# Expert weights of a mixture-of-experts stage in four 4 MB slots instead of eight 2 MB slots

## What is computed

```python
def ec_moe(h, w_router, w_gate, w_up, w_down):
    B, T, D = h.shape
    cap = EC_CAPACITY_FACTOR * T // N_EXPERTS
    logits = jnp.einsum('btd,de->bte', h, w_router).astype(jnp.float32)
    aff = jax.nn.softmax(logits, axis=-1)
    gate, idx = lax.top_k(jnp.swapaxes(aff, 1, 2), cap)
    xs = jax.vmap(lambda hb, ib: hb[ib])(h, idx)
    a = jnp.einsum('becd,edf->becf', xs, w_gate)
    u = jnp.einsum('becd,edf->becf', xs, w_up)
    y = jnp.einsum('becf,efd->becd', jax.nn.silu(a) * u, w_down)
    y = y * gate[..., None].astype(y.dtype)
    return jax.vmap(lambda ib, yb: jnp.zeros((T, D), yb.dtype).at[ib.reshape(-1)].add(yb.reshape(-1, D)))(idx, y)
```

## Time and profile before

| | |
|---|---|
| median of three runs | 1639.85 us |
| the profiled execution, its own time | 1641.37 us |
| its span, from the first to the last instruction | 1639.7 us |
| TensorE busy | 1493.5 us, 91% of the span |
| VectorE, ScalarE, GpSimd busy | 454.4, 274.3, 54.0 us |
| moved by DMA | 566.07 MB, 345 GB/s over the span |
| DMA in 830 to 1420 us | 428 GB/s |
| loads of expert weights | 184 of 2 MB and 16 of 1 MB |

### The profile page before, as it was taken

One profiled execution on the slowest core, in us unless ns is written; L12 is line 12 of the kernel. 1 busy time (PEld: TensorE's weight loads), 2 busy tenths in 40 slices (PEclk: granted clock), 3 DMA queues, 4 the chain that ended last, 5 costly groups with the idle time before them and its releaser, 6 DMA issues.

```text
span 1639.7 us, 19983 instructions
## 1 busy us (share of the span) xinstructions
PE 1493.5 (91%) x8345; PEld 908.4 (55%) x8345; DVE 454.4 (28%) x876; ACT 274.3 (17%) x412; POOL 54.0 (3%) x90
## 2 busy tenths in 40 slices
PE   4559999999999999799999998998998999999888
PEld 2138888887788999643534334344344335335345
DVE  3244552435446744600030030030020110300202
ACT  3032222323233322400000000000000000000002
POOL 0001000000001000300000000000000000000000
PEclk8779999999999999899999999999999999999999
DMA  8978878786663435689999999999999999999996
GB/s 355 428 299 299 300 265 282 243 293 225 222 227 95 127 123 230 253 343 428 428 427 428 428 428 429 428 428 428 428 428 428 428 428 428 428 428 428 421 406 236
DMA packets 106363, 566.07 MB, mean 345 GB/s; under 512 B 7932, under 2 KB 62404, under 8 KB 72132
## 3 DMA queue, kind: packets, MB, share of 16 engines
q1 hardware_dynamic: 93424, 497.04, 74.3%
q0 software_dynamic: 9216, 67.11, 11.5%
q10 hardware_dynamic: 3668, 1.12, 0.3%
HBM read 561.84 MB, written 3.41 MB: 345 GB/s over the span
## 4 chain that ended last, share of the span: by engine, by line
PE 64%; DMA 30%; DVE 4%; issue 1%; ACT 1%; ACTq 0%; DVEq 0%; SPq 0%
PE psum L440 62%; DMA ring<-in_w_up 25%; DMA ring<-in_w_ada 3%; DMA ring<-in_w_in 1%; DVE w_parts L1164 1%; DVE hid L1415 1%; DVE mix L1342 0%; DMA hid<-in_b_ada 0%; DVE ring L1152 0%; PE psum L452 0%; PE psum L573 0%; ACT w_parts L877 0%; PE psum L838 0%; PE psum L860 0%; PE psum L777 0%
## 5 line engine op out<-in xcount | busy, mean ns | idle before, releaser
L440 PE MATMUL psum<-ring,hid 128*64 128x512 f32 (+1 forms) x3200 | 677.7, 578 | 68.5 <-DMA ring<-in_w_up 53.6
L440 PEld LDWEIGHTS psum<-ring,hid 128*64 128x64 f32 x3200 | 246.3, 137 | 482.4 <-issue 384.7
L440 PE MATMUL psum<-h_parts,w_parts 128*128 128x384 f32 x1152 | 212.5, 339 | 0.0
L440 PEld LDWEIGHTS psum<-h_parts,w_parts 128*128 128x128 f32 x1152 | 199.2, 188 | 16.6 <-issue 15.9
L877 ACT ACTIVATE hid<-psum 128x512 f32<-128x512 f32 (+5 forms) x104 | 62.9, 624 | 684.7 <-PE psum L440 471.7
L1491 DVE TENSOR_TENSOR hid<-psum,hid 128x512 f32<-128x512 f32 x16 | 11.1, 692 | 599.9 <-PE psum L440 599.9
L1164 DVE TENSOR_TENSOR w_parts<-ring,w_parts 128x2048 fp32r<-128x2048 f32 x52 | 119.2, 2291 | 120.6 <-ACT w_parts L877 120.0
L440 PE MATMUL psum<-ring,early 128*32 128x512 f32 (+1 forms) x780 | 116.7, 676 | 34.1 <-DMA ring<-in_w_ada 34.0
L877 ACT ACTIVATE w_parts<-ring 128x2048 fp32r<-128x2048 f32 x52 | 99.4, 1912 | 252.6 <-PE psum L440 194.6
L440 PEld LDWEIGHTS psum<-w_parts,h_parts 128*128 128x128 f32 x864 | 107.5, 195 | 28.1 <-issue 27.3
L440 PE MATMUL psum<-w_parts,h_parts 128*128 128x256 f32 x864 | 112.6, 290 | 8.7 <-DVE h_parts L1199 8.7
(11 more groups left out here) (165 smaller groups left out, 531.3 us busy)
## 6 DMA issues: line engine op xcount, KB each, us to landing
ring<-in_w_gate SPq DMA_DIRECT2D x64, 2048.0 KB, 32.9
ring<-in_w_up SPq DMA_DIRECT2D x64, 2048.0 KB, 25.8
ring<-in_w_down SPq DMA_DIRECT2D x56, 2048.0 KB, 34.0
ring<-in_w_ada POOLq DMA_DIRECT2D x64, 1024.0 KB, 5.2
ring<-in_w_in SPq DMA_DIRECT2D x36, 1024.0 KB, 5.2
ring<-in_w_ada SPq DMA_DIRECT2D x16, 2048.0 KB, 16.5
ring<-in_w_out SPq DMA_DIRECT2D x16, 1024.0 KB, 5.5
ring<-in_w_down SPq DMA_DIRECT2D x16, 1024.0 KB, 15.1
```

The source lines that it names most:

```text
L440: return nc.tensor.matmul(out, lhsT, rhs, start=start, stop=stop, skip_group_check=True)
```

## The change

The eight slots become four double slots (`WIDE`), which begin at the slots 4, 6, 2 and 0 (`WIDE_AT`). A matrix is now cut into halves of 4 MB, 12 to a pair, and a half is one transfer, in which partition p gets eight consecutive gate or up rows or four consecutive down rows, 32 KB contiguous in HBM and in SBUF. Three things keep the old size: the very first loads, which fill the four double slots in eight transfers of 2 MB, in the old order of slots and with the old waits (`FIRST_LOADS`); the products, which are the same in number and shape; and the down matrices of the last pair, which keep their 16 transfers of 1 MB and have semaphores of their own now (`last_landed`).

What changes with the halves is who waits for what. TensorE waits for a whole half before its first product, and `moe_used` rises when the whole half has been used, so that the next load into it is issued then. The counts that ScalarE and VectorE wait for are rewritten to mean the same points. In `rows_copy_out` the copies write runs of 64 columns instead of 128, and read with a step of 8 instead of 4, since the rows on a partition are eight now.

```diff
 MATS = [("g", 0), ("u", 0), ("g", 1), ("d", 0), ("u", 1), ("d", 1)]
-PER_PAIR = 4 * len(MATS)
+PER_PAIR = 2 * len(MATS)
 RING = 8
+WIDE = RING // 2
+LAST = PER_PAIR * (PAIRS - 1)
 FIRST_BANKS = [1, 2, 5, 6]
 LAST_BANKS = [2, 3, 0, 1]
-ORDER = [4, 5, 6, 0, 2, 3, 7, 1]
+WIDE_AT = [4, 6, 2, 0]
+FIRST_LOADS = [4, 5, 6, 0, 2, 3, 7, 1]
...
-        moe_landed = [sem(f"moe_landed{n}") for n in range(RING)]
+        moe_landed = [sem(f"moe_landed{n}") for n in range(WIDE)]
+        last_landed = [sem(f"last_landed{n}") for n in range(4)]
...
-            def expert_load(pair, q):
-                what, e = MATS[q // 4]
-                part, slot = q % 4, ORDER[q % RING]
+            def expert_load(pair, q, sub=None):
+                what, e = MATS[q // 2]
+                part, slot = q % 2, WIDE_AT[q % WIDE]
                 if what == "d":
-                    src = down_rows[bass.ds(pair * 2 * FF + e * FF + part // 2 * BLK, BLK), :]\
-                        .rearrange("(p j) n -> p j n", j=4)[:, part % 2 * 2:part % 2 * 2 + 2, :]
-                    dst = ring[:, slot, :].rearrange("p (k n) -> p k n", k=2)
+                    src = down_rows[bass.ds(pair * 2 * FF + e * FF + part * BLK, BLK), :].rearrange("(p j) n -> p j n", j=4)
                 else:
-                    src = (gate_rows if what == "g" else up_rows)[bass.ds(pair * 2 * D + e * D + part * 512, 512), :]\
-                        .rearrange("(p k) n -> p k n", k=4)
-                    dst = ring[:, slot, :].rearrange("p (k n) -> p k n", k=4)
-                sp.dma_start(dst, src).then_inc(moe_landed[slot], 16)
-            def last_down_load(q):
-                e, part, slot = MATS[q // 4][1], q % 4, ORDER[q % RING]
+                    src = (gate_rows if what == "g" else up_rows)[bass.ds(pair * 2 * D + e * D + part * 1024, 1024), :]\
+                        .rearrange("(p k) n -> p k n", k=8)
+                rows = src.shape[1]
+                dst = ring[:, slot:slot + 2, :].rearrange("p s n -> p (s n)").rearrange("p (k n) -> p k n", k=rows)
+                lo, hi = (0, rows) if sub is None else (sub * rows // 2, (sub + 1) * rows // 2)
+                sp.dma_start(dst[:, lo:hi, :], src[:, lo:hi, :]).then_inc(moe_landed[q % WIDE], 16)
+            def last_down_load(q, sub):
+                e, part, slot = MATS[q // 2][1], q % 2 * 2 + sub, WIDE_AT[q % WIDE] + sub
                 for half in range(2):
                     first = (PAIRS - 1) * 2 * FF + e * FF + half * BLK
                     src = down_rows[first:first + BLK, part * BLK:(part + 1) * BLK].rearrange("(p j) n -> p j n", j=4)
                     dst = ring[:, slot, half * 4 * BLK:(half + 1) * 4 * BLK].rearrange("p (j n) -> p j n", j=4)
-                    sp.dma_start(dst, src).then_inc(moe_landed[slot], 16)
+                    sp.dma_start(dst, src).then_inc(last_landed[part], 16)
...
-            for q in range(RING):
-                if ORDER[q] == 7:
+            for slot in FIRST_LOADS:
+                if slot == 7:
                     sp.wait_ge(ada_free, 2 + 64)
-                if ORDER[q] == 0:
+                if slot == 0:
                     sp.wait_ge(lo_ready, U_ALL)
-                if ORDER[q] == 2:
+                if slot == 2:
                     sp.wait_ge(unit_used, U_ALL)
-                if ORDER[q] == 3:
+                if slot == 3:
                     sp.wait_ge(logits_done, 1)
-                if ORDER[q] == 1:
+                if slot == 1:
                     sp.wait_ge(routed, 1)
                     sp.wait_ge(h2_pool, len(H2_POOL))
-                expert_load(0, q)
+                expert_load(0, WIDE_AT.index(slot // 2 * 2), slot % 2)
             with sp.Fori(0, PAIRS - 1) as i:
                 for j in range(PER_PAIR):
                     sp.wait_ge(moe_used, PER_PAIR * i + (j + 1))
-                    expert_load(i + (j + RING) // PER_PAIR, (j + RING) % PER_PAIR)
-            for j in range(PER_PAIR - RING):
-                sp.wait_ge(moe_used, PER_PAIR * (PAIRS - 1) + j + 1)
-                if MATS[(j + RING) // 4][0] == "d":
-                    last_down_load(j + RING)
-                else:
-                    expert_load(PAIRS - 1, j + RING)
+                    expert_load(i + (j + WIDE) // PER_PAIR, (j + WIDE) % PER_PAIR)
+            for j, used in ((0, 1), (1, 2)):
+                sp.wait_ge(moe_used, LAST + used)
+                expert_load(PAIRS - 1, j + WIDE)
+            for j, used in ((2, 3), (3, 4)):
+                sp.wait_ge(moe_used, LAST + used)
+                for sub in range(2):
+                    last_down_load(j + WIDE, sub)
+            for j, used in ((4, 5), (5, 6)):
+                sp.wait_ge(moe_used, LAST + used)
+                expert_load(PAIRS - 1, j + WIDE)
+            for j, used in ((6, 7), (7, 9)):
+                for sub in range(2):
+                    sp.wait_ge(moe_used, LAST + used + sub)
+                    last_down_load(j + WIDE, sub)
...
-            def up_or_gate(slot, what, e, part):
-                for kk in range(4):
-                    k = 4 * part + kk
+            def up_or_gate(slot, what, e, part, sub):
+                for kk in range(4 * sub, 4 * sub + 4):
+                    k = 8 * part + kk
                     for half in range(2):
-                        off = kk * FF + half * BLK
+                        off = kk % 4 * FF + half * BLK
                         last = mm(bank[0 if what == "g" else 1][ES * half:ES * half + ES, :],
-                                  xs[:, k, e * ES:(e + 1) * ES], ring[:, slot, off:off + BLK], k == 0, k == KC - 1)
+                                  xs[:, k, e * ES:(e + 1) * ES], ring[:, slot + sub, off:off + BLK], k == 0, k == KC - 1)
                 return last
             def down(slot, e, part):
-                for jl in range(2):
-                    half, j = part // 2, part % 2 * 2 + jl
-                    rows = actT[:, j * P + half * ES:j * P + (half + 1) * ES]
+                for j in range(4):
+                    rows = actT[:, j * P + part * ES:j * P + (part + 1) * ES]
                     for c in range(4):
                         row = ES * (c % 2 ^ e)
-                        off = jl * D + c * BLK
-                        last = mm(bank[2 + c // 2][row:row + ES, :], rows, ring[:, slot, off:off + BLK],
-                                  part == 0 and jl == 0, part == 3 and jl == 1)
+                        off = j % 2 * D + c * BLK
+                        last = mm(bank[2 + c // 2][row:row + ES, :], rows, ring[:, slot + j // 2, off:off + BLK],
+                                  part == 0 and j == 0, part == 1 and j == 3)
...
-            def landed(i, q, more=0):
-                pe.wait_ge(moe_landed[ORDER[q % RING]], 48 * i + 16 * (q // RING + 1 + more))
+            def landed(i, q):
+                pe.wait_ge(moe_landed[q % WIDE], 48 * i + 16 * (q // WIDE + 2))
             def round_of(i, first=False, last_pair=False):
                 for q in range(PER_PAIR):
-                    what, e = MATS[q // 4]
-                    part, slot = q % 4, ORDER[q % RING]
+                    what, e = MATS[q // 2]
+                    part, slot = q % 2, WIDE_AT[q % WIDE]
                     start = first and e == 0
                     if part == 0 and what == "g":
                         if e == 0 and not first:
@@ -793,14 +807,6 @@
                             pe.wait_ge(xs_act, 2 * i + 2)
                         if not start:
                             pe.wait_ge(sil_ready, 2 * i + e)
-                    if first and q < 4:
-                        for quarter in ([0, 1], [2], [3], [])[q]:
-                            gather_quarter(quarter)
-                        if q == 0:
-                            pe.wait_ge(mod_rows_out, N_MOD)
-                            turn_mod(bank[2], act)
-                        pe.wait_ge(xs_dve if q % 2 else xs_act, q // 2 + 1)
                     if part == 0 and what == "u" and not start:
                         pe.wait_ge(act_ready, 2 * i + e)
                     if part == 0 and what == "d":
@@ -812,17 +818,34 @@
                         if not start:
                             pe.wait_ge(y_out, 2 * i + e)
                         turn_act(i, e)
-                    landed(i, q, e + 1 if last_pair and what == "d" else 0)
-                    if what != "d":
-                        last = up_or_gate(slot, what, e, part)
-                    elif last_pair and e == 1:
-                        last = down_block(slot, e, part, bank[LAST_BANKS[part]][:, 0:UC])
-                    elif last_pair:
-                        last = down_block(slot, e, part, bank[2 + part // 2][:, part % 2 * UC:(part % 2 + 1) * UC])
+                    if last_pair and what == "d":
+                        for sub in range(2):
+                            block = 2 * part + sub
+                            pe.wait_ge(last_landed[block], 32 * (e + 1))
```

(38 more changed lines are left out.)

6 lines of the change are left out of this document (1 added, 5 removed).

## The result

The changed kernel takes 1643.10 us (median of 22 runs, 1640.98 to 1645.54), the kernel before 1640.23 in the same comparison (22 runs, 1638.99 to 1641.43). The ratio is 1.0017, with a 95% interval of 1.001 to 1.0023: 1.6 to 3.8 us slower. I had forecast 0.4 us less and no measurable change. The range held the time, the direction was wrong: a small loss that twenty runs can tell from nothing.

What follows compares the result with a forecast made beforehand. The prediction took the end to be set by the weight stream's start, its rate and TensorE's work after the last up landing. +2.7 + 3.4 - 6.5 = -0.4 us on 1639.85 gave 1639.4 us, range 1636.4 to 1646.1.

Steps and rivals of the forecast that it cites:

- the start: First loads that wait for TensorE: released later in halves, making the stream 2.7 us late; bounds 0 and 4.9.
- 2.9 us ahead of 724.1: Second half's issue at 721.24 against the first half's landing; claimed to leave no gap or 0.1 us.
- the latency of an idle queue: Start of the stream: 3.0 us, from 7.9 us to land a 2 MB load less 4.9 for its bytes.
- The packets: Weight stream up to the last up half: 32 KB packets replace 16 KB ones and gain 6.5 us.
- The rows' price for a packet: DMA queue: about 9.5 ns per packet beside its bytes, from rates with 2 KB and 16 KB packets.
- the 2.5 us estimated by that page: Stream gain from fewer packets by the skill's rule of some 3 cycles each; sum would be +3.6 us.
- The tail: Behind the last up landing TensorE has two quarters to do, so the end comes 3.4 us later.
- The remark that it has no cover: Tail: nothing hides the 3.4 us and no other wait is ahead of it.
- The middle: Mid-stream: coarser waits and releases cost nothing, with 12.7 us of cover where 3.0 are needed.
- The rival of a queue that runs dry between releases: Middle up loads: late TensorE releases empty the DMA queue; one us more gives +6.6, 1646.4 us, slower; chance 0.05.
- +2.7 + 3.4 - 6.5: Whole kernel: late start plus longer tail less the packets' gain, summing to -0.4 us.
- the chance of 0.57 for no change: Whole kernel: chance given to the forecast of -0.4 us, with its own range of 1636.6 to 1643.1.

Runs made afterwards that it cites:

- 10 to 12: Follow-ups second_quarters, pad60, pad35, second_pad60 and the control, on what makes the second half land late; 1642.88, 1641.81, 1643.14, 1640.42 and 1640.25 us.
- the control: Kernel before with 60 small transposes put at the start of TensorE's program; 1640.25 us, ratio 1.0000 to the kernel before.
- pad60: Changed kernel with 60 small transposes at the start of TensorE's program, shifting its later instruction fetches; 1641.81 us, ratio 1.0015 to the kernel before.
- second_quarters: Changed kernel with only the second half behind the initial loads released and loaded in quarters; 1642.88 us, ratio 1.0015 to the kernel before.
- before_start: Kernel before with the first four loads behind the initial ones issued in twos, after two quarters are used; 1644.04 us, ratio 1.0025.
- pad35: Changed kernel with 35 small transposes at the start of TensorE's program, shifting its later instruction fetches; 1643.14 us, ratio 1.0017 to the kernel before.
- second_pad60: Changed kernel with the second half behind the initial loads in quarters and 60 transposes at TensorE's start; 1640.42 us, ratio 1.0002 to the kernel before.
- both_quarters: Changed kernel with the first two halves behind the initial loads and the last expert's up matrix in quarters; 1634.56 us, ratio 0.9968 to the kernel before.
- Both mended kernels: both_quarters with 32 KB pieces, 1634.56 us, and both_pieces16 with 16 KB pieces, 1639.84 us.
- before_tail: Kernel before with TensorE waiting for two quarters at once only in the last expert's up matrix; 1643.73 us, ratio 1.0025.
- tail_quarters: Changed kernel with the last expert's up matrix loaded and waited for in quarters; 1639.24 us, ratio 0.9994 to the kernel before.
- eighths: both_quarters with the last up quarter in two 1 MB transfers, the second waited for separately; 1634.55 us, ratio 0.9963 to the kernel before.
- before_mid: Kernel before with TensorE waiting for two quarters at once in all pairs but the last, behind the first eight quarters; 1640.50 us, ratio 1.0002.
- both_pieces16: both_quarters with every 4 MB half in two 2 MB transfers, so pieces are 16 KB; 1639.84 us, ratio 1.0000 to the kernel before.

## Why the prediction was wrong

**The step that failed is the start.** It said that the second half is issued "2.9 us ahead of 724.1, just the latency, so it follows with no gap or one of 0.1", and that the stream is late by 2.7 us. The issue times were right, the gap was not. The stream is late by 3.3 to 4.3 us in the traces, and by 4.2 us (2.5 to 5.9) when the releases alone are made coarse.

What took the place of that step is shown by 10 to 12, each from one trace. The later release by itself costs about what was forecast: 2.5 us against the control with the same transposes (starts of 32.1 and 29.6), 2.0 against the 30.1 of before, which holds a fetch's delay of its own. On top comes a gap of 1.0 to 2.2 us. The first half lands 12.1 us behind its issue, not 12.7, so the lead was 2.3 us and not 2.9. The gap is there with that short lead and no fetch near (`pad60`, 1.9 us), and with a fetch at the seam and a longer lead (`second_quarters`, 1.4; `before_start`, lead of 3.0, 1.6); with a lead of 3.5 and a fetch inside the first half (`pad35`) it is 1.0. It is gone when both are away (`second_pad60`). So the forecast of this term had no place for the fetches, and where they fall was luck.

How much a short lead costs by itself is less sure. The prediction called its 3.0 us the latency of an idle queue, but the load of the earlier trace rows that it was read from was issued at 711.36, 1.6 us before the one ahead had landed (704.92 and 8.0). It needed 7.9 us; the load that did meet an idle queue, at 704.92, needed 8.0. With 2 MB in pieces of 16 KB a short lead cost nothing, then, in the kernel before or in the control. And in `both_quarters` a 4 MB load issued at 726.45, a lead of 3.0, landed 9.7 us behind the one ahead, with no gap (though one late engine had held up that landing, too). Only `pad60` speaks for a cost of the short lead, with 4 MB in pieces of 32 KB: 13.9 us from issue to landing, where 9.7 are its bytes and an idle queue needs 12.2. Why is open.

**The packets: right in kind, somewhat too high.** 6.5 us were forecast. Both mended kernels, with 32 and 16 KB pieces, are 5.3 us apart (some 2.5 either way, so 6.5 is not excluded), and the streams of the traces with large packets are shorter by 6.0 us, a mean of 859.7 in eleven against 865.7 in seven. The rate is the forecast's 431 to 432 GB/s and the step from half to half is 9.71 us. What is missing may go to landings that come late by themselves, such as one of 10.9 us behind the last in the changed kernel near 783, with a fetch in the same stretch. That the fetches cause them is argued from where they stand, and from `pad35`, whose first half was 1.2 us late with a fetch inside it.

The rows' price for a packet, 9.5 ns, was the better guide than the 3 cycles that the Trainium skill gives in "DMA: Bandwidth & Descriptors", section "Why small descriptors are slow (HBM only)": the 2.5 us estimated by that page are half of the 5.3 measured, and less than half of the 6.0 by which the streams differ.

**The tail: right.** 3.4 us forecast, 3.4 in the traces, 3.9 (2.5 to 5.6) by the time of `before_tail`, 3.5 to 3.9 back in `tail_quarters`. The remark that it has no cover is confirmed, and `eighths` shows how near the next wait was in the other direction.

**The clock: not foreseen.** In the profiled execution the first column block ran 1.7 us longer with part of it at the half clock. It is in two of the eight profiles with the coarse tail and 32 KB pieces (the changed kernel's and `pad35`'s, there in the last up half), and in `before_start`, whose tail is not coarse. So it belongs to that execution and not clearly to the change. In the middle the change does bring half-clock stretches, behind waits of about 2.5 us, and `before_mid` shows that they are free there.

**The middle: right.** Nothing that could be measured is lost to coarser waits and releases (`before_mid`, `both_pieces16`). The rival of a queue that runs dry between releases did not occur.

**The sum.** Measured one by one: 4.2 for the start, 3.9 for the tail, -5.3 for the packets, +2.8 together, where the changed kernel is 2.9 slower. Each of the three is known to some 1.5 to 2.5 us only, so that they meet the total this closely is partly luck; in the profiled executions the time from TensorE's first product on is 4.7 us longer in the first, with 1.7 of it the clock, and 1.0 in the second. The prediction had +2.7 + 3.4 - 6.5. Each term had the right sign, and all three errors go the same way: 1.5 us for the start, 1.2 for the packets, 0.5 for the tail. The start's is the largest, but had the start cost the 2.7 of the forecast, the measured terms would still add up to +1.3. With three terms that cancel to -0.4, errors of this size decide the sign; the chance of 0.57 for no change said little of that.

## What to carry to other kernels

Where a queue of transfers sets the end, look at its three parts by themselves: a larger transfer gains in the stream, but it is released later at the start and waited for whole at the end. Keep both ends in small pieces and take the large ones only in the middle; here that turned 2.9 us of loss into 5.3 of gain, with a version that beats both kernels. Where a load is to follow without a gap and its lead comes out within a microsecond of the latency, count a gap of 1 to 2 us as well: a fetch of instructions at the seam is enough for it. And before a latency is called that of an idle queue, look when the transfer ahead landed.

## What the runs showed of the hardware

- A packet's own cost carries on to 32 KB pieces: 428 GB/s with 16 KB, 432 with 32 KB, where the price of 9.5 ns read from packets of 2 and 16 KB had given 431 to 432.
- From issue to landing a 4 MB transfer needs 12.0 to 12.2 us when the queue is idle, and needed 13.9 in the one trace where it was issued 2.3 us before the transfer ahead landed, with no fetch near (`pad60`). A 2 MB transfer issued 5.7 us ahead followed 4.9 us behind the one before it, with no gap (`second_pad60`).
- With one fetch of instructions inside it a transfer landed 1.2 us later (`pad35`, 13.4 and not 12.2), with a fetch at the seam 1.4 us (`second_quarters`), and in both 15 of its 16 small packets were on time and one was late. Where the fetches fall can be shifted by idle instructions far ahead (from 720.4 in the changed kernel to 717.5 with 35 transposes, and to 707.7 with 60).
- TensorE took 8.5 to 8.8 us instead of 7.1 for the same work behind a wait of 2.2 to 2.7 us in several traces, with a granted clock below 1 (`before_mid`, 0.83 in 885 to 895); but `second_quarters` waited 2.54 us, and `pad60` 3.45 and 2.66, and the halves behind took 7.09. The length of a wait is not enough to tell.
